# One plain FFN chunk becomes a block pair, and three pairs get two weight mixtures from ScalarE copies and adding transfers

## What is computed

```python
def swiglu(x, g, w_gu, w_down):                 # x: 576 x 1024, D_FF = 2816
    gu = rmsnorm(x, g) @ w_gu                   # 1024 -> 2 * 2816: gate | up
    return (jax.nn.silu(gu[..., :D_FF]) * gu[..., D_FF:]) @ w_down
...
        x = x + swiglu(x, g_ffn[i], w_gu[i], w_down[i])     # once in each of the two layers
```

## Time and profile before

| | |
|---|---|
| median of 3 runs | 1208.22 us (1208.21 to 1208.87) |
| the profiled execution's own time | 1208.02 us |
| its span in the trace | 1206.3 us |
| TensorE matmuls (PE) | 1197.1 us busy, 99% of the span |
| VectorE (DVE) | 979.7 us, 81% |
| ScalarE (ACT) | 641.6 us, 53% |
| GpSimd (POOL) | 78.5 us, 7% |
| chain that ended last | PE 93%, DVE 3%, ACT 1%, DMA 1%, issue 1% |

### The profile page before, as it was taken

One profiled execution on the slowest core, in us unless ns is written; L12 is line 12 of the kernel. 1 busy time (PEld: TensorE's weight loads), 2 busy tenths in 40 slices (PEclk: granted clock), 3 DMA queues, 4 the chain that ended last, 5 costly groups with the idle time before them and its releaser, 6 DMA issues.

```text
span 1206.3 us, 22717 instructions
## 1 busy us (share of the span) xinstructions
PE 1197.1 (99%) x8853; PEld 1152.8 (96%) x8853; DVE 979.7 (81%) x1585; ACT 641.6 (53%) x1136; POOL 78.5 (7%) x111
## 2 busy tenths in 40 slices
PE   8999999999999999999999999999999999999998
PEld 8998999999999999999987887899999999999998
DVE  5777458999999999976674777557999999999973
ACT  6657335455555555545672567434555555455543
POOL 2000000002001000102001100000001000100200
PEclk9999999999999999999999999999999999999999
DMA  7343222236334433526434110333134433532533
GB/s 249 108 140 105 71 78 83 74 89 136 106 88 113 121 97 91 133 80 173 137 107 140 57 41 2 105 88 88 53 101 115 120 97 94 130 105 80 131 85 105
DMA packets 195242, 124.08 MB, mean 103 GB/s; under 512 B 6339, under 2 KB 185891, under 8 KB 194880
## 3 DMA queue, kind: packets, MB, share of 16 engines
q1 hardware_dynamic: 183904, 103.30, 28.9%
q0 software_dynamic: 11040, 19.27, 7.4%
q10 hardware_dynamic: 192, 0.06, 0.0%
HBM read 106.70 MB, written 7.94 MB: 95 GB/s over the span
## 4 chain that ended last, share of the span: by engine, by line
PE 93%; DVE 3%; ACT 1%; DMA 1%; issue 1%; SPq 0%; DVEq 0%; ACTq 0%
PE ACCP L2016 28%; PE ACCP L2037 24%; PE MISC L2037 23%; PE ACCP L2173 3%; PE ACCP L2196 3%; PE ACCP L2366 2%; PE ACCP L2341 2%; PE MISC L2055 1%; PE MISC L2302 1%; PE MISC L2315 1%; DMA XR<-in_x_prompt 1%; PE MISC L2061 1%; PE ACCP L2078 1%; PE ACCP L2092 1%; DMA PC<-PC 0%
## 5 line engine op out<-in xcount | busy, mean ns | idle before, releaser
L1179 ACT ACTIVATE WH<-RAW 128x1024 fp32r<-128x1024 f32 (+2 forms) x149 | 144.2, 968 | 145.8 <-PE ACCP L2016 93.5
L1197 ACT ACTIVATE EH<-SB 128x1024 fp32r<-128x1024 f32 (+1 forms) x116 | 112.5, 970 | 163.2 <-DVE SB L1568 82.8
L1543 DVE TENSOR_TENSOR WL<-RAW,WH 128x1024 fp32r<-128x1024 f32 (+2 forms) x148 | 165.8, 1120 | 30.8 <-ACT WH L1179 29.7
L1574 DVE TENSOR_TENSOR EL<-SB,EH 128x1024 fp32r<-128x1024 f32 (+1 forms) x116 | 128.7, 1109 | 5.5 <-ACT EH L1197 3.7
L2037 PE MATMUL MISC<-BH,EH 128*128 128x288 f32 x360 | 106.7, 296 | 0.0
L2037 PE MATMUL ACCP<-BH,EH 128*128 128x288 f32 x360 | 106.6, 296 | 0.0
L2037 PE MATMUL MISC<-BL,EH 128*128 128x288 f32 x360 | 106.2, 295 | 0.0
L2037 PE MATMUL ACCP<-BL,EH 128*128 128x288 f32 x360 | 106.2, 295 | 0.0
L2037 PE MATMUL ACCP<-BH,EL 128*128 128x288 f32 x360 | 105.8, 294 | 0.0
L2037 PE MATMUL MISC<-BH,EL 128*128 128x288 f32 x360 | 105.8, 294 | 0.0
L2016 PE MATMUL ACCP<-XH,WH 128*128 128x288 f32 x480 | 104.1, 298 | 0.0
(11 more groups left out here) (411 smaller groups left out, 3432.0 us busy)
## 6 DMA issues: line engine op xcount, KB each, us to landing
RAW<-in_w_gu SPq DMA_DIRECT2D x88, 512.0 KB, 4.1
RAW<-in_w_down SPq DMA_DIRECT2D x48, 384.0 KB, 4.1
RAW<-in_w_in SPq DMA_DIRECT2D x16, 512.0 KB, 4.2
RAW<-in_w_mem_kv SPq DMA_DIRECT2D x16, 512.0 KB, 3.8
RAW<-in_w_out SPq DMA_DIRECT2D x16, 512.0 KB, 3.8
X<-PC POOLq DMA_DIRECT2D x48, 144.0 KB, 3.2
RAW<-in_w_down SPq DMA_DIRECT2D x16, 256.0 KB, 3.0
RAW<-in_w_kv SPq DMA_DIRECT2D x8, 512.0 KB, 3.6
```

Source lines behind the costliest of these rows:

```text
L1179: a.activation(panel_in(WH, w % SPLIT_SLOTS, p), panel_in(RAW, p % RAW_SLOTS, p), ACT.Copy).then_inc(split_ready(w, True)[0], 1)
L1197: a.activation(EH[:, first:first + n, 0:nh], mixtures(s)[:, first:first + n, 0:nh], ACT.Copy).then_inc(block_hi, n)
L1543: v.tensor_tensor(panel_in(WL, w % SPLIT_SLOTS, p), panel_in(RAW, p % RAW_SLOTS, p), panel_in(WH, w % SPLIT_SLOTS, p), ALU.subtract).then_ ...
L1574: v.tensor_tensor(EL[:, first:first + n, 0:nh], mixtures(s)[:, first:first + n, 0:nh], EH[:, first:first + n, 0:nh], ALU.subtract).then_in ...
```

## The change

One lead fewer (`LEADS` 3), so chunk 3 becomes the first pair and each layer has 31 pairs instead of 30. The first pair's panels are loaded after the second lead's, into two RAW slots that they hold through the leads; its mixtures 1 to 3 are made before the norm's scale is known and the fourth after two of the eight `prepare_scale`. The last token block's low part moves behind the last lead, between the first pair's EL. The hidden mixtures of chunks 0 and 1 move from the leads into the step of the second pair, those of chunks 2 and 3 into the step of the third.

For the second, third and fourth pair (`z` set), mixtures 1 and 2 of SB are no longer made by VectorE. ScalarE copies a quarter of the up panel into each (once with scale -1), in the step of the pair before, between `mix_hi_22` and `split_hi`; two adding transfers on POOL's queue, 256 KB each, then add the other quarter. VectorE's `blocks_lo` is put ahead of `mix_2` in these steps, and ahead of `mix_2` there is now a wait for the first transfer; ScalarE's `mix_hi` of the two mixtures waits for both.

```diff
-    LEADS = 4
+    LEADS = 3
+    BY_DMA = 3
...
-                   (1, 0): [("mix", 3), ("mix", 6), ("hi", 1), ("hi", 2)],
-                   (1, 1): [("lo", 0), ("lo", 1), ("hi", 3), ("hi", 4)],
-                   (2, 0): [("lo", 2), ("lo", 3), ("blocks", k0), ("hi", 5), ("hi", 6)],
-                   (2, 1): [("lo", 4), ("lo", 5), ("pair", count["pair"]), ("blocks_hi", k0)],
-                   (3, 0): [("lo", 6), ("blocks_lo", k0)], (3, 1): []}
+                   (1, 0): [("mix", 3), ("mix", 6), ("hi", 1), ("hi", 2), ("lo", 0)],
+                   (1, 1): [("lo", 1), ("lo", 2), ("hi", 3), ("hi", 4)],
+                   (2, 0): [("lo", 3), ("lo", 4), ("hi", 5), ("hi", 6)],
+                   (2, 1): [("lo", 5)]}
...
+                    add("prepare_pair", k=count["pair"], s=r_step.s)
                     add("prepare_scale", layer=layer, k=0)
                     add("prepare_scale", layer=layer, k=1)
+                    add("prepare_fourth", k=count["pair"])
...
-            if n == 1:
-                k = k0 + LEADS // 2 - 1
+            if n in (1, 2):
+                k = k0 + n - 1
...
 # POOL, step of a gate/up pair that is not late
+                    after = steps_of_pair[s.i + 1]
+                    if after.z is not None:
+                        k1, k2, nh = inputs_of(after)
+                        gp.wait_ge(*raw_there(after.p + 1))
+                        gp.wait_ge(mix_copied, 2 * after.z + 1)
+                        gp.dma_start(SB[:, 0, 0:nh], raw_panel(after.p + 1)[:, k2], accum_op=ALU.add).then_inc(first_mixed, 16)
+                        gp.wait_ge(*raw_there(after.p))
+                        gp.wait_ge(mix_copied, 2 * after.z + 2)
+                        gp.dma_start(SB[:, 1, 0:nh], raw_panel(after.p)[:, k1], accum_op=ALU.add).then_inc(second_mixed, 16)
                     gp.wait_ge(copied, 3 * s.i + 3)
                     gp.dma_start(PC[:, s.i % 2, 2], PC[:, s.i % 2, 1], accum_op=ALU.add).then_inc(kept_summed, 16)
...
 # ScalarE
+            def copy_for_sums(s, prev):
+                k1, k2, nh = inputs_of(s)
+                act.wait_ge(*raw_there(s.p + 1))
+                act.wait_ge(block_lo, 5 * prev.i + 2)
+                a.activation(SB[:, 0, 0:nh], raw_panel(s.p + 1)[:, k1], ACT.Copy).then_inc(mix_copied, 1)
+                a.activation(SB[:, 1, 0:nh], raw_panel(s.p + 1)[:, k1], ACT.Copy, scale=-1.0).then_inc(mix_copied, 1)
...
                     mix_hi_22(s)
+                    if s.nxt and steps_of_pair[s.i + 1].z is not None:
+                        copy_for_sums(steps_of_pair[s.i + 1], s)
...
 # VectorE, step of a pair
                         if s.k is not None:
                             mix_blocks(s.k)
-                    if after:
+                    by_dma = after and after.z is not None
+                    if after and not by_dma:
                         mix_1(after)
                         mix_3(after)
                     if not s.alone:
                         mix_lo_22(s)
+                    if by_dma and s.k is not None:
+                        blocks_lo(s.k)
                     if after:
                         mix_2(after)
-                    if s.k is not None:
+                    if not by_dma and s.k is not None:
                         blocks_lo(s.k)
                     if after:
                         mix_lo(after, 0, 2)
```

More of the change, by code:

```diff
@@ L325, in feed_forward @@
                     **panel((up_of if e else gate_of)(j), KC))
+                if (j, e) == (0, 1):
+                    first_pair = take("panel", 2)
+                    panel_shape.extend([(KC, P)] * 2)
+                    raw_free.extend([("pair", count["pair"])] * 2)
+                    add("load_first", p=first_pair, view=gate_of(LEADS), ys=up_of(LEADS))
                 for what, k in prepare[j, e]:
                     add("prepare_" + what, layer=layer, k=k)
+        for n in range(2):
+            slot_of[first_pair + 4 + n] = (first_pair + 2 + n) % RAW_SLOTS
+        last_lead = next(s for s in reversed(steps) if s.kind == "lead")
         order, waiting = [], []
@@ L360, in feed_forward @@
                 h=layer * FC + j if which == "gu" else None, prev=prev, nxt=n + 1 < len(order),
-                alone=n == 0, bank=n % 2, side=count["acc"] % 2, before=steps[-1] if n == 0 else None,
+                alone=n == 0, bank=n % 2, side=count["acc"] % 2, before=last_lead if n == 0 else None,
                 m=count["job"], g=count["acc"], made=made, k=k,
-                first=which == "down" and j == 0)
+                first=which == "down" and j == 0, z=take("summed") if 0 < n <= BY_DMA else None)
             steps_of_pair[i] = steps[-1]
@@ L832, in moving_of @@
             return {"x": (XH, XL, xl_ready, T), "y": (HH, HL, yl_ready, T)}[kind]
+        raw_slot, raw_before, users = [], [], [[] for _ in range(RAW_SLOTS)]
+        for p in range(len(panel_shape)):
+            slot = slot_of.get(p, p % RAW_SLOTS)
+            raw_slot.append(slot)
+            raw_before.append(users[slot][-1] if users[slot] else None)
+            users[slot].append(p)
         def panel_in(slots, slot, p):
@@ L876, in block_of, with mixtures_made @@
             return next(t[:, b - b0] for b0, b1, t in HBH[k] if b0 <= b < b1), HBL[k][:, b]
+        def mixtures_made(s, n):
+            own = sum(2 if steps_of_pair[i].z is not None else 4 for i in range(s.i))
+            if s.z is None:
+                return [(mixed, own + n)]
+            waits = [(first_mixed, 16 * (s.z + 1)), (second_mixed, 16 * (s.z + 1))][:n]
+            return waits + ([(mixed, own + n - 2)] if n > 2 else [])
         def mixtures(s):
@@ L1041, in _ @@
                         sp.dma_start(yp[:, 2:TT, D - P:D], YST[1][:, 2:TT]).then_inc(y_last_stored, 16)
-                elif s.kind == "pair":
+                elif s.kind == "load_first" or s.kind == "pair" and not s.alone:
                     load(s.p, s.view)
@@ L1191, in mix_hi @@
             def mix_hi(s, first, n):
-                act.wait_ge(mixed, 4 * s.i + first + n)
+                for made in mixtures_made(s, first + n):
+                    act.wait_ge(*made)
                 if s.i:
@@ L1945, in _ @@
                     mix_2(first)
-                    mix_4(first)
+                elif s.kind == "prepare_fourth":
+                    mix_4(steps_of_pair[s.k])
                 elif s.kind == "hl":
@@ L1953, in _ @@
                         dve.wait_ge(panel_used, s.before.q + 1)
-                        for n in range(4):
+                        for n in range(3):
                             mix_lo(s, n, 1)
+                        token_lo(s.layer, NB - 1)
+                        mix_lo(s, 3, 1)
                         mix_lo_22(s)
```

52 lines of the change are left out of this document (29 added, 23 removed).

## The result

The changed kernel takes 1223.5 us (median of 4 runs, 1222.55 to 1224.24) against 1208.22 for the kernel before beside it: 1.0128 of its time, 95% interval 1.0114 to 1.0141. The direction was as forecast. The size was not: +15.3 us where +7.4 had been summed, and above the range's end of 1219.5. The profiled execution took 1223.63 us, its span 1221.9.

The account below looks back on a forecast made before the run. TensorE was taken to bound the kernel, with VectorE just behind. Stops of 6.4 us a layer (5.8 + 0.6), 12.8 in two, less 2.16 of earlier stops and 3.2 of matmuls, made +7.4: 1215.5 us, range 1211.5 to 1219.5.

Parts of the forecast that it names:

- Pair 0's step: Copies, then transfers: second issued at 4.4, landing in 4.5 (range 2.6 to 5.7), first `cross` 12.7 us after pair 0's start.
- The rounds: VectorE, pairs 1 and 2, cross to cross: 11.49 plus waits of 1.07 for WH and 1.48 for HBH, 14.04 us each.
- The landings of the later two steps: Transfers issued some 2 us into the rounds of pairs 1 and 2: landing of 4.5 leaves 4 us cover, 5.7 fits.
- Pair 3's HBL and the third sum: HBL ends 9.8 us after pair 3's cross, at 50.6; with a third sum (0.47), TensorE waits 0.6 in the first down pair.
- The matmuls and the leads: Twelve fewer matmuls save 1.60 us a layer, 3.2 in both; leads shrink by 12.8 to 39.2 us without a stop.
- Pair 0's stop of 0.24: TensorE's stop in pair 0 was to go, because VectorE no longer comes late out of HBL.
- pair 1 near 11.2: Sign in TensorE's windows: pair 1 near 11.2 us, pair 2 near 13.2, pair 3 near 13.7.
- rival (a): Transfers decide: second landing of 2.6 gives 1212.6, 5.7 gives 1217.9 (forecast's stops, 0.70); slower transfers or copies 1219.5 and over, 0.13.
- (b): Rival: faster, VectorE doesn't wait; break-even at rounds of 12.2, rounds of 11.5 give 1203 to 1205; chance 0.07.
- (c): Rival: no change to be told, one of VectorE's two waits mostly absent, rounds near 12.4, 1208 to 1210; chance 0.08.
- (d): Rival: the clock falls in TensorE's stops, a pair takes 11.2 us more, 1230 and beyond; chance 0.02.

Follow-up runs that it names:

- the two experiments on order: Against the changed kernel: one puts `mix_2` and `mix_4` ahead of HBL, 1217.7 us; the other puts ScalarE's copies behind WH and the silu, 1223.5 us.

## Why the prediction was right and wrong

**The step that failed** is in "Pair 0's step": "I take 4.5, between the ends", for the second transfer's landing, with 5.7 as the upper bound. It landed in 7.67 and 7.46. The first cross came at 16.28 and 16.09 instead of 12.7, 3.6 and 3.4 us late, and VectorE carried that unchanged to the end of pair 3's HBL: 7.0 of the 7.8 us by which the stops (20.6) exceed the forecast's 12.8. The prediction saw that the transfer "meets SP's two panels for pair 2", and still bounded it by the 5.7 of the earlier trace rows, a landing beside the same panels, but of one transfer of 144 KB, and one of only two such landings in that trace (4.16 in layer 0, 5.65 in layer 1). That bound failed twice over. It was too low for the same 144 KB transfer, which landed in 7.0 and 7.2 beside the panels in two of the experiments. And the work is larger: by the DMA view of 231 to 242 of the kernel before, the transfer and the panels took 8.4% and 32.6% of 11 us, 0.9 and 3.6 us of the 16 engines; three transfers of 0.67 MB in place of 0.15 make 4.1 us at that rate, and with the panels 7.7. That this sum meets the landing is no rule, as the 7.0 with 4.6 us of work shows.

The cause is the panels on the same engines. The experiment that holds them brought the landing back to 4.07 and the cross to 12.70 in layer 1, and to 5.72 and 14.33 in layer 0, where the rest stays open; the one without pair 1's transfers took 7.1 us off. That SP's panels make the transfer late, and that this is the miss, is shown; how the engines divide their time between the two is not.

The Trainium skill bears on it twice. DMA: Bandwidth & Descriptors, section Anatomy of one DMA — SWDGE (gpsimd) path, would give an estimate of 2.6 us for 256 KB; the runs show 3.2 for a first transfer on quiet engines, 4.1 for a second issued 0.55 us behind it, and 7.7 beside the panels. The same page, section Issuing engines are not separate DMA queues, says that transfers of all issuing engines end up on the same 16 DMA engines and interleave. The two rows of queues above agree: q0 and q1 are on the engines in the same stretch, 4.5 and 3.7 us of them.

**The rounds** were right: 14.09 for 14.04, the waits 1.06 for 1.07 and 1.35 for 1.48, put where they were forecast, and each removed by one of the two experiments on order. **The landings of the later two steps** hide, as argued: no wait of VectorE on a transfer there. **Pair 3's HBL and the third sum**: 9.77 for 9.8 after the cross, a handover of 0.15 that was left out, and 0.66 and 1.01 for 0.6; why layer 1 has 1.01 stays open (with the panels held it has 1.01 too, at a granted clock of 1.00). **The matmuls and the leads**: 39.20 us without a stop, as said.

**Smaller misses.** "Pair 0's stop of 0.24 should go". It stayed in both layers. The reason given was VectorE's lateness out of HBL; the row at 214.71 shows EL waiting 0.95 for ScalarE's EH instead. It adds nothing, as VectorE sets the end of these pairs anyway. The low part among pair 0's EL was counted as "one token block's low part" out of the leads and nowhere else; without transfers it costs 1.8 us, and with them it should be hidden behind the late landing, which no run tests. The profile's windows were misjudged with the sum: pair 1 near 11.2 was forecast, and it took 13.95, because the cross is late already there. Two readings were off without weight in the sum: VectorE's round in pair 2's step before took 11.96 us (crosses at 250.69 and 262.65), so it lost 0.8 there and not 1.5 "again"; and rival (a)'s cross at 11.6 makes stops of 5.3 a layer by the prediction's own sum, not 5.0.

**The rivals.** The far end of (a) is what happened, at a landing beyond its ends. (b) needed rounds of 12.2: with the order mended they are 11.74 to 12.0, and with pair 1 left out the time is 1205.1, so the mechanism of (b) was there for the taking, but not in this order. (c) did not come: neither wait was absent. (d) came in small. The windows of layer 1's pair 2, cut at the clock, show it:

```profile
889.73:893.50 3.77, 1.94 (x15) 1.70 (x14) 3.77 (x4) 0.75 (x2) 0.00 (x0) 1.00 0.84 250
893.50:896.90 3.40, 3.40 (x15) 3.40 (x16) 3.00 (x5) 2.84 (x5) 0.08 (x1) 0.50 0.02 6
896.90:904.54 7.64, 7.64 (x59) 7.64 (x58) 5.42 (x8) 5.06 (x8) 2.51 (x3) 1.00 0.66 125
```

For 3.4 us the granted clock is 0.50, the lower level of 1.2 GHz. It cost nothing: pairs 2 and 3 together take 14.81 + 14.18 = 28.99 us in layer 1 and 14.09 + 14.90 = 28.99 in layer 0, where the clock stays at 1.00. VectorE set the pace, and TensorE used up time that it would have waited.

## What to carry to other kernels

When work moves to DMA, look at everything that is on the engines in that stretch, loads of other queues included, instead of taking a landing from another place as the bound: here three adding transfers (4.5 us of all engines) and two panels (3.7) went together with a second landing of 7.7 us where 4.1 is the quiet price. The sum of engine times is a first estimate and no bound, as one small transfer beside the panels took 7.0. Give an engine's new short tasks a place behind what another engine waits for, unless a late start is dear (in pair 0's step the same move cost 1.9 to 2.8 us), and fill the waits with what is ready: with the step in which they collide left out, the same transfers lost 4.9 us in the change's order and gained 4.0 in the other. And follow the first late event: here a delay ahead of the engine that already set the pace was never made up, and counted in full at the end.

## What the runs showed of the hardware that was not expected

- An adding transfer of 256 KB from SBUF into SBUF landed in 3.2 us, a second one 0.55 us behind it in 4.1, on quiet engines; together with two 512 KB panels the first took 4.0 to 7.8 and the second 7.35 to 9.2. A 144 KB one alone beside the panels took 4.15 to 7.21 in the kernel before and the four variants that have it so. The panels paid too: 6.8 us in the stretch above against the page's median of 4.2. And adding bytes are dear: 0.67 MB held the 16 engines for 3.8 us in the quiet step, the panels' 1.05 MB for 3.7.
- With the panels away from pair 0's step, the second took 5.7 and 5.9 in the two cases where an instruction packet of 16 KB occupied one engine for 1.5 to 1.8 us among them, and 4.1 in the two where it lay ahead of them. That the packet caused it was not tested by itself.
- The lower clock came after a stop of TensorE of 2.13 us, start to start, at 893.33 (changed kernel), after 2.13 with the panels held, 2.58 with `mix_4` early, and 4.81 with the copies later, where it also came inside a stop of 3.79. It did not come after three stops of 2.06 to 2.22 us in layer 0 of the changed kernel, nor after two of 2.21 with transfers for the third and fourth pair alone. So in these runs the length of the stop alone doesn't tell.
